# A two-layer decoder trunk with expert retrieval: TensorE adds up each batch of v rows one tick later

## The chip, the core and the metric

The kernel runs on one core of a Trainium2 chip. The metric is the device time of one execution in microseconds (us), lower is better. All data are float32.

## What is computed

The reference runs `DEPTH` = 2 layers over one sequence of 256 tokens of width 1024. A layer has a mixing half (normalisation, one input projection, three groups of attention heads, an output projection) and an expert half, the part that this case is about:

```
def peer_ffn(h, wq, subkeys, u_tab, v_tab):
    ...
        q = (hc @ wq).reshape(PEER_CHUNK, PEER_HEADS, 2, PEER_HALF)
        s = jnp.einsum('thcd,hcnd->thcn', q, subkeys).astype(jnp.float32)
        sv, si = lax.top_k(s, PEER_TOPK)
        ...
        fv, fpos = lax.top_k(cand, PEER_TOPK)
        eidx = jnp.take_along_axis(cidx, fpos, axis=-1)
        gate = jax.nn.softmax(fv, axis=-1)
        u = jnp.take(u_tab, eidx, axis=0)
        act = jnp.einsum('thkd,td->thk', u, hc).astype(jnp.float32)
        coef = (gate * jax.nn.gelu(act, approximate=False)).astype(hc.dtype)
        vsel = jnp.take(v_tab, eidx, axis=0)
        return jnp.einsum('thk,thkd->td', coef, vsel)
```

Each token picks 16 of 16,384 experts for each of 8 heads, 128 in all. An expert has a row u and a row v of 1024 numbers. The output of a token is the sum of its 128 v rows, each weighted by gate x gelu(u . h).

## The kernel before

**Phases, ticks and rows.** The 256 tokens are two tiles of 128, so there are `PHASES` = 4 phases, one for each layer and tile. The first 300 us compute the modulation vectors and the mixing half of phase 0. From then on the engines do the expert half of phase `ph` and, beside it, the mixing half of phase `ph + 1`. A phase has 64 ticks, each of `BATCH` = 2 rows. A "row" k is one gathered transfer: for each of the 128 tokens of the tile the u and the v of its k-th expert, 128 x 2048 float32, 1,048,576 bytes. In this text "tick 72" counts through all phases (phase 1 is ticks 64 to 127), and "weigh 72" is the TensorE work on the rows of tick 72.

**The ring.** Rows land in `ringmem`, a ring of 9 slots. GpSimd (POOL) issues them in order (L368), each as soon as its slot is free: row k uses the slot of row k - 9. What a row goes through: it lands; VectorE (DVE) multiplies u with h and sums (`row`, L1418, 1.2 us); after both rows of the tick ScalarE (ACT) applies gelu (L1015); DVE multiplies with the gate (L1431); ACT builds two diagonal matrices, one a row (L1023, semaphore `diag_ready`); TensorE (PE) multiplies each with its v row and adds it up in PSUM (`weigh`, L760, two matmuls a row). The last of these frees the slot.

**The mixing half beside it** is cut into 79 segments. `pace()` deals them out over the ticks from the numbers in `COST`; tick m does the segments up to `PACE[m]`. Each engine has its own list of what it does in a segment, written as a generator and moved on by `Pace.upto`. Every engine runs strictly in program order. The order inside a tick is, on DVE: two `row`s, part of a retrieval, the segments of the tick, the coefficients; on ACT: gelu, the segments, the diagonals; on PE: the segments, then `weigh` of the same tick. At tick 0 of a phase there is no segment, in phase 3 there are next to none.

The segments fall in four stretches of a phase: ticks 1 to 19 the input projection (L401, L404), whose weight groups SP loads one by one when PE is through with the group before the last (L311); ticks 19 to 36 attention and the pairwise products (L471, L484 to L552), with many round trips between PE and DVE inside a tick; ticks 37 to 48 the state sums (L585 to L614) and the output projection (L623); ticks 49 to 60 the queries (L636) and scores (L648). At the last tick PE also puts the next tile's h into PSUM (`place_h`, L750), for which it waits until DVE is done with all dot products of the phase. At tick 0 DVE takes the sums of the phase before out of PSUM (`add_sum`, L1439), for which it waits for the last weigh of that phase.

Of the kernel before, what the change touches and what calls it, by code (L numbers as in the profile page):

```python
# [38 lines left out]
TICKS = SEL // BATCH  # L39
PHASES = DEPTH * NT  # L40
# [97 lines left out]
def trunk(nc, x, c, final_norm_g, ada_pairs, w_groups, w_pieces, param_cols, param_rows, lora_w, subkeys_t, peer_uv,  # L138
# [4 lines left out]
    with ExitStack() as ctx:  # L143
# [123 lines left out]
        def slot(k):  # L267
            return ringmem[:, (ADA_SLOTS + k) % RING, :]
# [5 lines left out]
        def freed(k):  # L274

            q = ADA_SLOTS + k
            return slot_free[q % RING], q // RING + 1
# [16 lines left out]
        with nc.Block() as block:  # L294
# [78 lines left out]
            def _(pe):  # L373
# [365 lines left out]
                def last_gate():  # L739
                    for n in range(2):  # L740
                        yield 75 + n
                        gate_row(g_at(PHASES, n), gdiag[1], bank[6],
                                 ("g_sb", g_at(PHASES, n)) if n else ("q_sb", at("q_sb", PHASES, 0)))

                def place_h(ph):

                    if ph:
                        pe.wait_ge(s["dots_done"], TICKS * ph)
                    for k in range(KD):
                        tr = nc.tensor.transpose(hrep[:, k * P:(k + 1) * P], hT[:, k, :], ident)  # L750
                    tr.then_inc(s["hrep_out"], 1)

                def weigh(n):
                    pe.wait_ge(s["diag_ready"], n + 1)
                    if n % TICKS == 0 and n:
                        pe.wait_ge(s["sums_taken"], n // TICKS)
                    for k in range(n * BATCH, (n + 1) * BATCH):
                        for b in range(2):
                            q = slice(b * 512, (b + 1) * 512)
                            mm = nc.tensor.matmul(acc[:, q], diag[:, k % DIAGS, :], slot(k)[:, D:][:, q],  # L760
                                                  start=(k % SEL == 0), stop=(k % SEL == SEL - 1), skip_group_check=True)
                        mm.then_inc(freed(k)[0], 1)
# [3 lines left out]
                for ph in range(PHASES):  # L766
                    beside = Pace(mixing(ph + 1) if ph + 1 < PHASES else last_gate())
                    for m in range(TICKS):
                        beside.upto(PACE[m])
                        if m == TICKS - 1 and ph + 1 < PHASES:  # L770
                            place_h(ph + 1)
                        weigh(ph * TICKS + m)

            @block.scalar
            def _(act):
# [15 lines left out]
                def mixing(i):  # L791
# [24 lines left out]
                    def take(name):  # L816
                        g = NUMBER[name]
                        _, _, w, kind = GROUPS[g]
                        act.wait_ge(s["proj_out"], at("proj_out", i, g + 1))
                        src = group_bank(g)[:, 0:w]  # L820
                        if name == "dq":

                            for a in range(2):
                                ins = nc.scalar.activation(dq[:, a].rearrange("p j c -> p (j c)"), src, ACT.Copy,
                                                           scale=const["halves"][:, a:a + 1])
                            ins.then_inc(s["proj_sb"], 1)
                            return
                        if name in SHIFTED:
                            a, b = SHIFTED[name]
                            dst = colsT[:, a:b, 1:]  # L830
                        else:
                            dst = places[name]
                        if kind == "f":
                            src = src.rearrange("p (j c) -> p j c", c=P)
                        nc.scalar.activation(dst, src, ACT.Copy).then_inc(s["proj_sb"], 1)
# [719 lines left out]
```

## Time and profile before

| | |
|---|---|
| median of 3 runs (lowest to highest) | 1921.21 us (1920.2 to 1927.48) |
| the profiled execution | 1921.61 us |
| its span, first to last instruction | 1919.8 us |
| busy: PE / DVE / ACT / POOL | 85% / 74% / 34% / 27% |
| read from memory | 703.64 MB, 367 GB/s over the span |

The profiled execution lies 0.4 us above the median. Its phases begin with the dot products at about 307, 735, 1158 and 1585 us: three phases with mixing beside them take some 425 us each, and the last, without it, 325 us.

### The profile page before, as it was taken

How to read it: one execution, taken by the hardware profiler on the slowest of the kernel's cores; microseconds unless marked ns; L12 is line 12 of the kernel's file. 1: busy time of each engine (PE TensorE's matmuls, PEld its weight loads, DVE VectorE, ACT ScalarE, POOL GpSimd, SP SyncE). 2: the span in 40 equal slices, each digit the busy share in tenths (PEclk: the TensorE clock that was granted, in tenths of full speed). 3: DMA queues.
4: the chain of work that ended last, by engine and by line, in shares of the span. 5: the costliest groups of instructions: out<-in, count | busy, mean ns of one | idle time of the engine just before them, and what ended most of it. 6: DMA issues, size and time to landing. Idle time of an engine off the chain costs nothing.

```text
span 1919.8 us, 20976 instructions
## 1 busy us (share of the span) xinstructions
PE 1627.2 (85%) x6868; PEld 1017.1 (53%) x6868; DVE 1429.6 (74%) x3407; ACT 656.2 (34%) x1591; POOL 514.3 (27%) x564
## 2 busy tenths in 40 slices
PE   0768686998999997998999998998999998887786
PEld 0757674564556664564665664654565663333332
DVE  5768578866998666867997757868987758777754
ACT  1222123433543333433642334334642333222222
POOL 2000003222232332232232232222223333433331
PEclk9888688999999999999999999999999998999999
DMA  9963688998799999999799999998799999999995
GB/s 392 407 275 115 235 326 329 405 406 333 257 364 383 421 422 399 408 414 353 274 392 390 420 421 401 401 418 296 268 375 407 420 421 418 421 421 421 420 419 245
DMA packets 96989, 706.08 MB, mean 368 GB/s; under 512 B 10992, under 2 KB 11504, under 8 KB 13296
## 3 DMA queue, kind: packets, MB, share of 16 engines
q0 software_dynamic: 80640, 587.24, 76.6%
q1 hardware_dynamic: 16240, 117.50, 15.1%
q8 instruction: 55, 0.90, 0.2%
q14 instruction: 54, 0.44, 0.1%
HBM read 703.64 MB, written 1.05 MB: 367 GB/s over the span
## 4 chain that ended last, share of the span: by engine, by line
PE 44%; DVE 30%; DMA 18%; issue 5%; ACT 3%; POOL 0%; DVEq 0%; ACTq 0%; POOLq 0%
PE psum L760 24%; DMA ringmem<-in_peer_uv_dram,eidx 13%; DVE ringmem L1418 7%; PE psum L401 6%; PE psum L636 4%; DMA W<-in_w_groups_dram 3%; PE psum L623 3%; DMA ringmem<-in_ada_pairs_dram 2%; PE psum L404 2%; DVE ringmem L1052 2%; DVE W L1182 1%; PE psum L736 1%; ACT diag L1023 1%; DVE attn L1192 1%; DVE ast L1193 1%
## 5 line engine op out<-in xcount | busy, mean ns | idle before, releaser
L760 PE MATMUL psum<-ringmem,diag 128*128 128x512 f32 x2048 | 974.4, 623 | 124.8 <-ACT diag L1023 124.5
L368 POOL DMA_INDIRECT ringmem<-in_peer_uv_dram,eidx x512 | 488.6, 954 | 1132.3 <-PE psum L760 1086.5
L1418 DVE SCALAR_TENSOR_TENSOR ringmem<-ringmem,psum 128x1024 f32<-128x1024 f32 x512 | 613.2, 1220 | 176.6 <-DMA ringmem<-in_peer_uv_dram,eidx 162.9
L760 PEld LDWEIGHTS psum<-ringmem,diag 128*128 128x128 f32 x2048 | 391.2, 199 | 594.0 <-issue 413.0
L1023 ACT ACTIVATE diag<-K,coef 128x128 f32<-128x128 f32 x512 | 176.3, 392 | 255.3 <-DVE coef L1431 255.2
L401 PE MATMUL psum<-hT,W 128*128 128x128 f32 x1344 | 170.0, 284 | 44.3 <-DVE hT L1144 20.4
L401 PEld LDWEIGHTS psum<-hT,W 128*128 128x128 f32 x1344 | 166.8, 200 | 68.7 <-issue 41.4
L1015 ACT ACTIVATE coef<-dots 128x2 f32<-128x2 f32 x256 | 51.8, 202 | 369.6 <-DVE ringmem L1418 365.0
L1052 DVE SCALAR_TENSOR_TENSOR ringmem<-ringmem,diag 128x1024 f32<-128x1024 f32 x96 | 115.8, 1224 | 23.2 <-DMA pcols<-in_param_cols_dram 13.4
L636 PEld LDWEIGHTS psum<-hT,W 128*128 128x128 f32 x1024 | 123.3, 197 | 11.7 <-issue 7.7
L636 PE MATMUL psum<-hT,W 128*128 128x128 f32 x1024 | 126.1, 281 | 2.3 <-ACT hT L809 2.3
L1431 DVE SCALAR_TENSOR_TENSOR coef<-coef,ginv,gexp 128x2 f32<-128x2 f32 x256 | 56.7, 221 | 74.8 <-ACT coef L1015 68.5
L1015 ACT ACT_TABLE_LOAD x80 | 102.6, 1283 | 1.4
L359 POOL DMA_DIRECT2D ringmem<-in_ada_pairs_dram x48 | 25.5, 537 | 242.5 <-DVE ringmem L1052 241.7
L854 ACT ACTIVATE attn<-attn,ast 128x128 f32<-128x128 f32 (+1 forms) x64 | 28.7, 449 | 122.9 <-DVE ast L1194 122.9
L623 PE MATMUL psum<-W,hT 128*128 128x256 f32 x256 | 60.6, 394 | 2.0 <-issue 2.0
L623 PEld LDWEIGHTS psum<-W,hT 128*128 128x128 f32 x256 | 50.4, 198 | 15.9 <-issue 9.1
L383 PE MATMUL psum<-K,hm 128*128 128x128 f32 x96 | 15.4, 313 | 39.1 <-ACT hm L804 27.6
L985 ACT ACTIVATE ar<-psum 128x256 f32<-128x256 f32 x32 | 12.3, 383 | 103.9 <-PE psum L636 97.4
L404 PE MATMUL psum<-W,hT 128*128 128x260 f32 (+1 forms) x128 | 40.9, 465 | 6.0 <-DMA W<-in_w_groups_dram 6.0
L1165 DVE TENSOR_TENSOR W<-psum,K 128x512 f32<-128x512 f32 x24 | 16.6, 691 | 37.2 <-PE psum L471 36.7
L1418 DVE DVE_READ_ACCUMULATOR ringmem<-ringmem,psum 128x1 f32 x512 | 42.3, 83 | 0.0
(245 smaller groups left out, 1652.1 us busy)
## 6 DMA issues: line engine op xcount, KB each, us to landing
ringmem<-in_ada_pairs_dram POOLq DMA_DIRECT2D x48, 1024.0 KB
W<-in_w_pieces_dram SPq DMA_DIRECT2D x48, 1024.0 KB
W<-in_w_groups_dram SPq DMA_DIRECT2D x24, 1536.0 KB
W<-in_w_groups_dram SPq DMA_DIRECT2D x12, 1024.0 KB
ringmem<-in_peer_uv_dram,eidx POOLq DMA_INDIRECT x512
W<-in_w_groups_dram SPq DMA_DIRECT2D x4, 1040.0 KB
attn<-in_subkeys_t_dram SPq DMA_DIRECT2D x4, 1024.0 KB
K<-in_consts_dram SPq DMA_DIRECT2D x1, 1546.0 KB, 19.1
```

Of the source, the lines that this page charges most:

```text
L368: nc.gpsimd.indirect_dma_start(slot(k), None, rows, bass.IndirectOffsetOnAxis(ap=eidx[:, ph % 2, m:m + 1], axis=0)).then_inc(row_landed[q ...
L401: mm = nc.tensor.matmul(group_bank(g)[:, j * P:(j + 1) * P], wt[:, k, j * P:(j + 1) * P], hT[:, k, :], start=(k == 0), stop=(k == KD - 1))
L404: mm = nc.tensor.matmul(group_bank(g)[:, 0:w], hT[:, k, :], wt[:, k, 0:w], start=(k == 0), stop=(k == KD - 1))
L623: mm = nc.tensor.matmul(bank[6 + j // 2][:, (j % 2) * 256:(j % 2 + 1) * 256], hT[:, k, :], wpiece[j % 3][:, k, :], start=(k == 0), stop=(k ...
L636: mm = nc.tensor.matmul(bank[6 + h % 2][:, a * P:(a + 1) * P], wpiece[j % 3][:, k, a * P:(a + 1) * P], hT[:, k, :], start=(k == 0), stop=( ...
L760: mm = nc.tensor.matmul(acc[:, q], diag[:, k % DIAGS, :], slot(k)[:, D:][:, q], start=(k % SEL == 0), stop=(k % SEL == SEL - 1), skip_grou ...
L854: ins = nc.scalar.activation(sc[:, n % 2, a, 0:nk], sc[:, n % 2, a, 0:nk], exp, bias=ast[:, n % 2, a:a + 1], scale=DIFF_SCALE if kind == " ...
L1015: nc.scalar.activation(coef[:, q], dots[:, q], gelu).then_inc(s["gelu_out"], 1)
L1023: ins = nc.scalar.activation(diag[:, k % DIAGS, :], ident, ACT.Copy, scale=coef[:, j:j + 1])
L1052: ins = v.scalar_tensor_tensor(out=u, in0=u, scalar=1.0, in1=crow, op0=ALU.mult, op1=ALU.mult, accum_out=MC[:, l, SECTIONS[r // KD], r % K ...
L1418: ins = v.scalar_tensor_tensor(out=u, in0=u, scalar=1.0, in1=hrep, op0=ALU.mult, op1=ALU.mult, accum_out=dots[:, j:j + 1])
L1431: step(v.scalar_tensor_tensor(out=coef[:, q], in0=coef[:, q], scalar=ginv[:, ph % 2, h:h + 1], in1=gexp[:, ph % 2, m * BATCH:(m + 1) * BAT ...
```

## The change

The call of `weigh` takes the rows of the tick before, so that on PE the rows of tick n are added up behind the segments of tick n + 1. The last weigh of all comes behind the loop.

```diff
                         beside.upto(PACE[m])
                         if m == TICKS - 1 and ph + 1 < PHASES:
                             place_h(ph + 1)
-                        weigh(ph * TICKS + m)
+                        if ph or m:
+                            weigh(ph * TICKS + m - 1)
+                weigh(PHASES * TICKS - 1)
```

On PE, at the start of phase 0, the program before has this (L750 is `place_h`, L760 x4 one weigh, L383 and L401 the segments of tick 1 and on):

```order
 L750 MATMUL psum<-K,hT 128x128 x8
 L760 MATMUL psum<-ringmem,diag 128x512 x4
 L383 MATMUL psum<-K,hm 128x128 x8
 L401 MATMUL psum<-hT,W 128x128 x8
 L760 MATMUL psum<-ringmem,diag 128x512 x4
```

and the changed one this:

```order
 L750 MATMUL psum<-K,hT 128x128 x8
 L383 MATMUL psum<-K,hm 128x128 x8
 L401 MATMUL psum<-hT,W 128x128 x8
 L760 MATMUL psum<-ringmem,diag 128x512 x4
 L401 MATMUL psum<-hT,W 128x128 x8
```

The first L760 row has gone from before L383 to behind L401. From here on every place of a weigh holds the one with the next lower number: no row moves, each L760 row stands for the tick before. With the waits shown this can be seen where a phase ends. Before, on PE at the end of phase 0 (the weigh that also waits for `sums_taken` is the first one of a phase):

```order
 L760 MATMUL psum<-ringmem,diag 128x512 [waits diag_ready]
 L760 MATMUL psum<-ringmem,diag 128x512 x3
 L750 MATMUL psum<-K,hT 128x128 [waits dots_done]
 L750 MATMUL psum<-K,hT 128x128 x7
 L760 MATMUL psum<-ringmem,diag 128x512 [waits diag_ready]
 L760 MATMUL psum<-ringmem,diag 128x512 x3
 L760 MATMUL psum<-ringmem,diag 128x512 [waits sums_taken,diag_ready]
 L760 MATMUL psum<-ringmem,diag 128x512 x3
 L383 MATMUL psum<-K,hm 128x128 [waits score_sb,h_ready]
 L383 MATMUL psum<-K,hm 128x128 x7
```

and after the change:

```order
 L750 MATMUL psum<-K,hT 128x128 [waits dots_done]
 L750 MATMUL psum<-K,hT 128x128 x7
 L760 MATMUL psum<-ringmem,diag 128x512 [waits diag_ready]
 L760 MATMUL psum<-ringmem,diag 128x512 x3
 L760 MATMUL psum<-ringmem,diag 128x512 [waits diag_ready]
 L760 MATMUL psum<-ringmem,diag 128x512 x3
 L383 MATMUL psum<-K,hm 128x128 [waits score_sb,h_ready]
 L383 MATMUL psum<-K,hm 128x128 x7
 L401 MATMUL psum<-hT,W 128x128 [waits w_in0,hT_dve,hT_act]
 L401 MATMUL psum<-hT,W 128x128 x7
 L760 MATMUL psum<-ringmem,diag 128x512 [waits sums_taken,diag_ready]
```

Behind `place_h` there now stand the last two weighs of the old phase, and the first of the new one (`sums_taken`) stands behind L383 and L401. The other engines' programs are as they were.

## Rows read from the trace of the kernel before

**Rows 1.** The page's groups: the weigh's matmuls, and the row transfers' issues.
```profile
L760 PE MATMUL psum<-ringmem,diag 128*128 128x512 f32 x2048 | 974.4, 623 | 124.8 <-ACT diag L1023 124.5
L368 POOL DMA_INDIRECT ringmem<-in_peer_uv_dram,eidx x512 | 488.6, 954 | 1132.3 <-PE psum L760 1086.5
```

**Rows 2.** Stretches: length, busy us of PE, PEld, DVE, ACT, POOL; granted clock; DMA share; GB/s.
```profile
868.00:964.00 96.00, 88.08 (x369) 52.77 (x370) 82.95 (x220) 50.99 (x115) 26.31 (x28) 0.95 0.85 310
...
1012.00:1160.00 148.00, 139.37 (x596) 87.04 (x595) 101.61 (x243) 44.75 (x121) 45.18 (x48) 0.99 1.01 414
1160.00:1176.00 16.00, 9.56 (x22) 4.07 (x20) 9.12 (x23) 6.16 (x13) 3.75 (x4) 0.79 1.02 423
1176.00:1184.00 8.00, 7.38 (x41) 5.39 (x42) 7.29 (x20) 3.38 (x9) 1.87 (x2) 1.00 0.83 311
...
1600.00:1900.00 300.00, 236.26 (x495) 96.25 (x494) 214.27 (x502) 77.07 (x219) 110.10 (x117) 0.93 1.01 418
```

**Rows 3.** DVE's waits for PE's first pair products, at 430:600, 860:1010, 1290:1430.
```profile
DVE W L1165 <- PE psum L471: 8.0, 2, 6.0
...
DVE W L1165 <- PE psum L471: 6.2, 2, 4.2
...
DVE W L1165 <- PE psum L471: 7.4, 2, 5.3
```

**Rows 4.** The chain of waits, 740 to 870 us: start, us, what.
```profile
804.24 5.40 PE psum L760 x8
...
859.00 9.19 DMA W<-in_w_groups_dram
```

**Rows 5.** PE in order of time, ticks 101 to 104 of phase 1.
```profile
992.05 3.60 PE L760 MATMUL psum<-ringmem,diag 128*128 128x512 f32 x8
...
1003.74 3.60 PE L760 MATMUL psum<-ringmem,diag 128*128 128x512 f32 x8
...
1012.76 3.70 PE L760 MATMUL psum<-ringmem,diag 128*128 128x512 f32 x8
1019.15 5.40 PE L760 MATMUL psum<-ringmem,diag 128*128 128x512 f32 x8 [2.68 <-ACT diag L1023]
```

**Rows 6.** POOL in order of time at the same place.
```profile
995.92 0.94 POOL L368 DMA_INDIRECT ringmem<-in_peer_uv_dram,eidx  x1 [0.51 <-PE psum L760]
1005.89 0.94 POOL L368 DMA_INDIRECT ringmem<-in_peer_uv_dram,eidx  x1 [9.04 <-PE psum L760]
```

**Rows 7.** Two stretches of 8 us at the same place, columns as in rows 2.
```profile
1000.00:1008.00 8.00, 7.80 (x35) 5.29 (x34) 7.69 (x19) 6.64 (x16) 1.32 (x2) 0.83 0.98 385
1008.00:1016.00 8.00, 8.00 (x50) 6.01 (x49) 3.44 (x9) 1.34 (x2) 1.48 (x2) 1.00 0.94 333
```

**Rows 8.** PE in order of time, from phase 1 to phase 2.
```profile
1157.25 1.09 PE L750 MATMUL psum<-K,hT 128*128 128x128 f32 x8 [1.19 <-DVE ringmem L1418]
1158.46 3.70 PE L760 MATMUL psum<-ringmem,diag 128*128 128x512 f32 x8
1167.65 6.53 PE L760 MATMUL psum<-ringmem,diag 128*128 128x512 f32 x8 [5.48 <-ACT diag L1023]
1174.01 1.04 PE L383 MATMUL psum<-K,hm 128*128 128x128 f32 x8
1176.62 2.02 PE L401 MATMUL psum<-hT,W 128*128 128x128 f32 x16 [1.58 <-ACT hT L809]
```

**Rows 9.** DVE in order of time there: the sums of phase 1 are taken.
```profile
1163.93 1.23 DVE L1439 TENSOR_TENSOR hm<-psum,grow 128x1024 f32<-128x1024 f32 x1
```

**Rows 10.** POOL in order of time there, and a transfer in the chain of waits.
```profile
1162.44 0.94 POOL L368 DMA_INDIRECT ringmem<-in_peer_uv_dram,eidx  x1 [0.78 <-PE psum L760]
1171.70 0.94 POOL L368 DMA_INDIRECT ringmem<-in_peer_uv_dram,eidx  x1 [8.33 <-PE psum L760]
...
1144.76 16.16 DMA ringmem<-in_peer_uv_dram,eidx
```

**Rows 11.** A transfer among few others: 512 KB, us from issue to landing.
```profile
diag<-in_c_dram SPq DMA_DIRECT2D x1, 512.0 KB, 4.8
```

## Prediction

> **What bounds the kernel now.** I read the page first, then the stretches, then the waits, then single engines in order of time.
>
> The page says who waits for whom: POOL, which issues the row transfers, sat idle 1132 us, 1086 of them for PE's weigh (L760), while PE waited for diagonals (ACT L1023) only 124.5 us in all [rows 1]. So rows are issued when slots come free, and the weigh frees them.
>
> The stretches say where that matters. A row of 1,048,576 bytes takes 2.49 us at the 421 GB/s or so that the transfers reach. In phase 1 the 148 us from 1012 on run at 414 GB/s with the DMA engines busy throughout, and so does nearly all of phase 3 (418) [rows 2]. There a phase can only be as fast as its bytes. From 868 to 964 us, the attention segments, DMA moves only 310 GB/s; DVE is busy 82.95 us of 96 and PE 88.08 [rows 2]: the engines are the limit, rows wait in the ring. The other two phases have the same pattern. What the change is worth is thus: how much earlier or later do slots come free at the point (about 1010 us in phase 1) from which the transfers run without a pause to the end of the phase? Time won before that point counts only if it brings the weighs forward.
>
> **The change part by part.** It removes nothing and adds no instruction. All 2048 L760 matmuls stay, and a weigh takes 3.6 us as before [rows 5]. In the program of PE every place of a weigh holds the one of the tick before.
>
> *Gain: PE no longer stops for a diagonal that is just being made.* At tick 72 PE had idled and its weigh took 5.40 us (804.24, at the lower clock for a part) instead of 3.7; behind it the chain of waits is PE alone down to the load of the last weight group (859.00, 9.19 us), after which come the first pair products [rows 4]. In the changed kernel weigh 71 stands there, which is ready, and the segments of tick 73 are done in what was idle. All projection segments behind it come some 5 to 7 us earlier (a weigh of 3.6 less before each, plus about 2 of clock), and with them that load and the pair products L471. DVE waits for these 8.0, 6.2 and 7.4 us, 21.6 in three phases, 7.2 a phase [rows 3]. This is the most that can be won there: after it DVE is the limit.
>
> *Nothing in the attention segments.* There PE's segment of a tick needs DVE's results of the same tick, so the place of each weigh stays where it is in time. Only its number changes: slots come free a tick later. Rows have landed long before they are used there (310 of 421 GB/s), which covers it.
>
> *Loss 1: the start of phases 1 and 2.* Before, weigh 128 starts at 1167.65, after a wait of 5.48, takes 6.53 at the lower clock, and fits in front of the turn L383 (1174.01), which is held up by the new tile's normalisation anyway [rows 8]; the granted clock of that stretch is 0.79 [rows 2]. Now it stands behind L383 and L401, in the place at 1176.62 + 1.9 = 1178.5. Besides, `place_h` (ends 1158.3) now precedes two weighs instead of one, so weigh 127 ends at 1158.3 + 2 x 3.6 = 1165.5, and DVE, which takes the sums at 1163.93 without waiting [rows 9], starts 1.6 us later; the place of weigh 128 becomes 1180.1. Its first row frees a slot after half of it, at 1181.9 or so, instead of 1171.7 [rows 10]: 10 us later. The queue of transfers does not cover all of this. The row issued at 1144.76 lands 16.16 later, at 1160.9 [rows 10]; the seven issued after it up to 1162.44 last 7 x 2.49 us more, to 1178.3. The next would be issued at 1182, and a transfer needs about 3.5 us beside its own bytes (estimate from 512 KB in 4.8 us, of which 1.25 are the bytes [rows 11]), so bytes flow again at 1185.5: 7.2 us dry. Before, 1176 to 1184 ran at 311 GB/s, that is 2.1 us dry [rows 2]. Net 5.1 us less of row traffic, in a stretch that otherwise runs full, so the rows of the projection ticks come up to 5.1 us later, and DVE reaches the pair products that much later. The PE path (1.6 us for the sums, some 2 for L401 at the lower clock) is shorter and runs beside it. Bounds: 0, if rows wait long enough in the ring, and 10, the whole delay of the issue. I take 5.1, and the same for phase 0, where the first weigh moves likewise. So DVE enters the attention segments at -7.2 + 5.1 = -2.1 us, between -7.2 and +2.8.
>
> *Loss 2: the end of the light stretch.* At ticks 101 to 104 the places of the weighs are far apart: 992.05, 1003.74, 1012.76, then 1019.15 after an idle 2.68 [rows 5]. POOL had no slot from 996.9 to 1005.89, 9.04 us [rows 6], and yet the transfers kept going (385 and 333 GB/s from 1000 to 1016, together 2.4 us dry [rows 7]): what was issued at 995.92 came in front of the gap. In the changed kernel weigh 101 is in the place of 1003.74 and weigh 102 in that of 1012.76. The two rows that went out just before the gap come only behind it, and the queue runs out about 2 x 2.49 us before its former end of 1008, near 1003; with an issue at 1005.9 bytes flow at 1009.4. That is 6.4 us dry where 0.7 were, 5.7 more. At 1016 weigh 103 follows at once and the spacing is nearly as before; from here on the transfers run full to the end of the phase, so the 5.7 is not won back. Bounds: 0, if weight loads fill the hole, and 9.0, the whole gap of POOL. I take 5.7. By the same amount as DVE is early, this place is early.
>
> By row, a phase changes by -2.1 + 5.7 = +3.6 us, and three by +10.8. Phase 3 has no segments between its weighs, its order is the same and it is bound by bytes. 1921.6 + 10.8 = 1932.4; I put 1933.
>
> The Trainium skill (DMA: Bandwidth & Descriptors, Anatomy of one DMA, SWDGE path) gives a transfer a fixed cost of about 2.0 us beside its bytes. By that each dry spell would be 1.5 us shorter, a phase +0.6, and the sum 1923. The only comparable row here has 3.5, on another queue and at the start of the kernel; no row shows a lone gathered transfer.
>
> **The rivals.**
>
> *No change worth measuring.* The gain is whole and the first loss is covered (rows of ticks 68 to 74 lie waiting in the ring), so a phase is -7.2 + 5.7 = -1.5, or both halves are smaller: 1917 to 1927, say 1922. For it: a full ring holds 22 us of traffic. Against it: DMA runs full over the projection ticks, so what is lost there isn't made up before the attention segments.
>
> *Faster.* DVE's 21.6 us of waits go, and the hole at 1003 is filled by the output projection's weight loads, which SP issues when PE gets there, earlier than before: 1921.6 - 21.6 = 1900; with a half of it 1911. It decides if rows issued at 995.92 and before aren't what keeps DMA busy up to 1008. Against it: in the 16 us from 1000 to 1016 those loads were there too, and 2.4 us stayed dry.
>
> *Much slower: the ring is too short throughout.* Slots are held a tick (425/64 = 6.6 us) longer, of the 16.16 that a row now takes from issue to landing [rows 10] some 9.5 are left, and where the weighs come in uneven steps the queue empties again and again. The full stretches are three phases of 425 us, each less the 144 from 868 to 1012, 843 us at about 414 GB/s [rows 2]; if they fell to the 385 GB/s of the eight us before the gap at 1008 [rows 7], that would be 843 x (414/385 - 1) = 63 us, 1985; half of it 1953. The Trainium skill (Perfetto Trace Analysis, Identifying Performance Opportunities) says that gaps which repeat can mean too few buffers, which is this case. Against it: a queue of 16 us is nearly three times what a transfer seems to need (3.5 + 2.49), and PE's places are some us early.
>
> **How the numbers follow.** I give 0.45 to the forecast (its own range 1926 to 1942), 0.25 to no change (1917 to 1927), 0.12 to faster (1900 to 1914) and 0.18 to much slower (1943 to 1985). The range leaves out the faster half of the third and the slower half of the last: 1910 to 1953. About 0.5%, 9.6 us, is what a measurement of this kernel can tell from no change. From the cases: above 1930.8 the last case and two thirds of the first, 0.18 + 0.31 = 0.49, and a little of the second, 0.5; below 1911.6 0.11 and a little more from the second, 0.13; the rest 0.37.
>
> **What the profile after would show.** Right: PE's waits for ACT L1023 before L760 fall well below 124.5 us; DVE's waits for L471 nearly vanish; at the starts of phases 1 and 2 L383 comes without a weigh before it and POOL has a gap of 15 us or more; the 16 us about the weighs 101 to 103 move less than 385 and 333 GB/s, and dot products of ticks 114 to 128 wait for transfers as before. POOL's time without a slot grows. Wrong: if GB/s over the full stretches fell everywhere, the ring rival holds; if these stretches are as full as before and begin earlier, the gain was whole. What would upset the sum most is the first loss: if DVE enters the attention segments 7 us earlier, the whole comes out near no change.

## The result, and the profile after

The changed kernel takes 1964.81 us (median of 4 runs, 1961.01 to 1972.42), the kernel before 1922.24 beside it (4 runs, 1920.2 to 1927.48): a ratio of 1.0233, with a 95% interval of 1.021 to 1.0257, slower. The prediction was 1933, within 1910 to 1953. It had the sign at even odds and the size wrong: 11 us were forecast, 43 came.

The profiled execution has a span of 1959.2 us (before: 1919.8). In the changed kernel lines behind L771 have numbers higher by 2: L1420 is the dot product L1418, L1025 the diagonals L1023, L1441 the sums L1439, L806 and L811 are L804 and L809. The trace has two records for each matmul of a weigh, so its four stand as x8. From the changed kernel's page, the groups that answer to [rows 1], and the dot products (columns: busy us, mean ns | idle us ahead, and what ended most of it):

```profile
L760 PE MATMUL psum<-ringmem,diag 128*128 128x512 f32 x2048 | 959.2, 616 | 66.4 <-ACT diag L1025 66.3
L1420 DVE SCALAR_TENSOR_TENSOR ringmem<-ringmem,psum 128x1024 f32<-128x1024 f32 x512 | 616.3, 1220 | 292.1 <-DMA ringmem<-in_peer_uv_dram,eidx 285.2
L368 POOL DMA_INDIRECT ringmem<-in_peer_uv_dram,eidx x512 | 489.9, 957 | 1178.4 <-PE psum L760 1124.0
```

PE waits for diagonals half as long as before, 66.3 us, and all of that lies in phase 3: from 300 to 1600 us, where it was 63.1 in the kernel before, the wait is gone. Another has grown: DVE's dot products wait 285.2 us for rows (162.9 in the kernel before), and POOL sits idle 46 us longer ahead of its issues, of which 37.5 are put down to a slot that PE has not freed.

Stretches of the changed kernel, columns as in [rows 2]. The first three are the state sums and what follows them in phase 1, from tick 103 on (answering to [rows 7] and the 148 us of [rows 2]), the next three the start of phase 2, the last is in phase 3:

```profile
1012.00:1028.00 16.00, 15.74 (x92) 12.70 (x93) 9.40 (x24) 7.98 (x17) 1.86 (x2) 0.89 0.79 303
1028.00:1036.00 8.00, 6.56 (x16) 2.62 (x14) 7.58 (x17) 2.48 (x5) 3.73 (x4) 1.00 0.99 391
1036.00:1184.00 148.00, 134.82 (x574) 85.85 (x575) 93.65 (x227) 42.05 (x116) 42.92 (x45) 0.97 0.99 404
...
1184.00:1200.00 16.00, 6.18 (x19) 3.28 (x17) 8.26 (x20) 5.31 (x11) 3.39 (x4) 0.73 0.98 407
1200.00:1208.00 8.00, 6.42 (x25) 4.66 (x24) 7.31 (x21) 3.93 (x10) 0.67 (x1) 0.69 0.01 4
1208.00:1216.00 8.00, 8.00 (x46) 5.66 (x45) 5.60 (x13) 2.36 (x7) 3.08 (x4) 1.00 0.86 306
...
1635.00:1935.00 300.00, 231.03 (x488) 94.51 (x487) 214.49 (x511) 76.20 (x216) 112.03 (x118) 0.94 1.01 419
```

Measured against 421 GB/s, the start of phase 2 is dry for 0.5 + 7.9 + 2.2 = 10.6 us. For eight of them nothing moves at all (4 GB/s). The 24 us from 1012 on are dry for 4.5 + 0.6 us, and the 148 us after it run at 404 where they ran at 414. Phase 3 is as full as before (419 and 418).

PE in order of time from phase 1 to phase 2, answering to [rows 8]:

```profile
1172.23 8.00 PE L760 MATMUL psum<-ringmem,diag 128*128 128x512 f32 x16
1180.56 1.09 PE L750 MATMUL psum<-K,hT 128*128 128x128 f32 x8 [0.33 <-DVE ringmem L1420]
1181.49 7.03 PE L760 MATMUL psum<-ringmem,diag 128*128 128x512 f32 x16
1198.34 1.97 PE L383 MATMUL psum<-K,hm 128*128 128x128 f32 x8 [9.82 <-ACT hm L806]
1201.88 3.46 PE L401 MATMUL psum<-hT,W 128*128 128x128 f32 x16 [1.58 <-ACT hT L811]
1205.18 3.60 PE L760 MATMUL psum<-ringmem,diag 128*128 128x512 f32 x8
```

POOL in order of time there, answering to [rows 10]:

```profile
1188.79 0.94 POOL L368 DMA_INDIRECT ringmem<-in_peer_uv_dram,eidx  x1 [0.78 <-PE psum L760]
1207.33 0.94 POOL L368 DMA_INDIRECT ringmem<-in_peer_uv_dram,eidx  x1 [17.61 <-PE psum L760]
```

and DVE, answering to [rows 9]:

```profile
1188.61 1.23 DVE L1441 TENSOR_TENSOR hm<-psum,grow 128x1024 f32<-128x1024 f32 x1 [1.42 <-issue]
```

Behind the two weighs of the old phase PE idles 9.82 us, and then L383 takes 1.97 us (1.04 before) and L401 3.46 (2.02 before), with a granted clock of 0.69 in the stretch. Only then comes the weigh of the new phase. POOL had no slot for 17.61 us.

How the lag grows can be read off the starts of the dot products in DVE's order of time. The table gives, for the first dot product of some ticks, how much later than in the kernel before it starts (us; negative is earlier), in one profiled execution each, with the difference at tick 0 taken off. The kernels beside the changed one are those of the experiments.

| tick | changed | e4, first weigh late | e7, place_h first | e3, 37 to 62 late | e11, 2 to 21 late | e15, 7 slots |
|---|---|---|---|---|---|---|
| 8 | +6.9 | +6.5 | 0.0 | 0.0 | -2.9 | +5.3 |
| 36 | -1.7 | +6.1 | -0.1 | -0.2 | -11.8 | +6.2 |
| 64 | +9.3 | +5.5 | +0.9 | +14.4 | -12.1 | +16.9 |
| 72 | +19.1 | +11.6 | +4.1 | +13.4 | -13.6 | +20.6 |
| 84 | +19.6 | +12.9 | +4.8 | +13.4 | -14.8 | +27.8 |
| 100 | +13.2 | +11.9 | +3.7 | +12.1 | -21.0 | +27.2 |
| 128 | +26.0 | +11.3 | +4.2 | +24.6 | -20.0 | +43.7 |
| 136 | +35.2 | +17.9 | +8.8 | +23.0 | -21.2 | +46.4 |
| 164 | +29.7 | +18.3 | +9.9 | +23.8 | -28.0 | +57.9 |
| 192 | +36.1 | +16.5 | +5.9 | +33.8 | -27.9 | +67.5 |
| 255 | +39.6 | +16.5 | +9.4 | +35.2 | -28.4 | +79.2 |

In the changed kernel each phase gains 5 to 9 us in its attention ticks and ahead of them (8 to 36: -8.6, 84 to 100: -6.4, 136 to 164: -5.5), loses 7 to 10 at its start (0 to 8: +6.9, 64 to 72: +9.8, 128 to 136: +9.2), and 6 to 13 from tick 36 to its end (36 to 64: +11.0, 100 to 128: +12.8, 164 to 192: +6.4). These are three quantities, and the experiments take them one by one. "us by ratio" below is the measured ratio less 1, times 1920; the 95% interval of each such number reaches some 3 to 6 us to either side (10 for e15).

### The profile page after: what moved, and what is told of

The parts are those of the page before. It is cut to its first block, busy times and chain, and to the rows that moved or that the text cites. A ratio compares the mean times of both kernels' runs of the same rounds, so it can differ in the third digit from the quotient of the medians.

```text
span 1959.2 us, 20976 instructions
## 1 busy us (share of the span) xinstructions
PE 1625.6 (83%) x6868; PEld 1023.7 (52%) x6868; DVE 1429.8 (73%) x3407; ACT 654.9 (33%) x1591; POOL 515.6 (26%) x564
## 3 DMA queue, kind: packets, MB, share of 16 engines
q1 hardware_dynamic: 16240, 117.50, 14.8%
## 4 chain that ended last, share of the span: by engine, by line
PE 46%; DVE 25%; DMA 22%; issue 4%; ACT 3%; POOL 0%; DVEq 0%; ACTq 0%; POOLq 0%
PE psum L760 24%; DMA ringmem<-in_peer_uv_dram,eidx 19%; DVE ringmem L1420 6%; PE psum L401 5%; PE psum L636 5%; PE psum L623 3%; DVE ringmem L1054 2%; DMA ringmem<-in_ada_pairs_dram 2%; PE psum L404 2%; DMA W<-in_w_groups_dram 2%; PE psum L736 1%; DVE attn L1194 1%; DVE ast L1195 1%; DVE W L1167 1%; DVE W L1184 1%
## 5 line engine op out<-in xcount | busy, mean ns | idle before, releaser
L760 PE MATMUL psum<-ringmem,diag 128*128 128x512 f32 x2048 | 959.2, 616 | 66.4 <-ACT diag L1025 66.3
L1420 DVE SCALAR_TENSOR_TENSOR ringmem<-ringmem,psum 128x1024 f32<-128x1024 f32 x512 | 616.3, 1220 | 292.1 <-DMA ringmem<-in_peer_uv_dram,eidx 285.2
L760 PEld LDWEIGHTS psum<-ringmem,diag 128*128 128x128 f32 x2048 | 388.9, 198 | 523.9 <-issue 413.9
L1025 ACT ACTIVATE diag<-K,coef 128x128 f32<-128x128 f32 x512 | 176.4, 392 | 286.1 <-DVE coef L1433 285.9
L401 PE MATMUL psum<-hT,W 128*128 128x128 f32 x1344 | 172.0, 286 | 42.3 <-DVE hT L1146 20.4
L401 PEld LDWEIGHTS psum<-hT,W 128*128 128x128 f32 x1344 | 169.1, 202 | 66.6 <-issue 41.1
L636 PEld LDWEIGHTS psum<-hT,W 128*128 128x128 f32 x1024 | 123.3, 197 | 15.1 <-ACT hT L811 7.9
L383 PE MATMUL psum<-K,hm 128*128 128x128 f32 x96 | 19.9, 375 | 92.6 <-ACT hm L806 74.6
L383 PEld LDWEIGHTS psum<-K,hm 128*128 128x128 f32 x96 | 15.7, 193 | 100.0 <-ACT hm L806 56.9
L1420 DVE DVE_READ_ACCUMULATOR ringmem<-ringmem,psum 128x1 f32 x512 | 42.3, 83 | 0.0
## 6 DMA issues: line engine op xcount, KB each, us to landing
ringmem<-in_peer_uv_dram,eidx POOLq DMA_INDIRECT x512, 11.2
```

Of the source, the lines that this page charges most:

```text
L383: tr = nc.tensor.transpose(bank[4 + b][:, j * P:(j + 1) * P], hm[:, (4 * b + j) * P:(4 * b + j + 1) * P], ident)
L401: mm = nc.tensor.matmul(group_bank(g)[:, j * P:(j + 1) * P], wt[:, k, j * P:(j + 1) * P], hT[:, k, :], start=(k == 0), stop=(k == KD - 1))
L636: mm = nc.tensor.matmul(bank[6 + h % 2][:, a * P:(a + 1) * P], wpiece[j % 3][:, k, a * P:(a + 1) * P], hT[:, k, :], start=(k == 0), stop=( ...
L1025: ins = nc.scalar.activation(diag[:, k % DIAGS, :], ident, ACT.Copy, scale=coef[:, j:j + 1])
L1420: ins = v.scalar_tensor_tensor(out=u, in0=u, scalar=1.0, in1=hrep, op0=ALU.mult, op1=ALU.mult, accum_out=dots[:, j:j + 1])
```

## The experiments

All but two of these kernels keep the order of the segments and change only which weighs are late. The loop of the changed kernel is written with a count of the weighs done, so that late ones are caught up where the condition ends:

```diff
+                added = [0]
...
+                        n = ph * TICKS + m
+                        late = ph < PHASES - 1 and 8 <= m <= 21
                         if m == TICKS - 1 and ph + 1 < PHASES:
                             place_h(ph + 1)
-                        weigh(ph * TICKS + m)
+                        while added[0] < (n if late else n + 1):
+                            weigh(added[0])
+                            added[0] += 1
```

**e1, the end and the start of a phase as before.** Here and in e3 and e6 the last tick also does the weigh that is still open ahead of `place_h`:

```diff
+                        late = ph < PHASES - 1 and 1 <= m <= 62
+                        if m == TICKS - 1:
+                            weigh(added[0])
+                            added[0] += 1
```

> The changed order inside a phase (ticks 1 to 62 late), but the end and the start of a phase as before: weigh 62 ahead of place_h, weigh 63 behind it, and the new phase's first weigh ahead of L383. Theory A (the price is paid at places: some 10.5 us a phase at its start, 11.5 from the end of the pair products to the phase's end, against a gain of 7 to 8): 1965 less 3 x 10.5 = 1933, within 1926 to 1942. Theory B (the ring is short by a tick everywhere, so the price is spread over all ticks with late weighs): 2 of 64 ticks are restored, 1960 to 1965.

Measured: 1936.38 us, ratio 1.0091 (1.0061 to 1.012), +17 by ratio. Theory A's number. Of the 45 us that the change costs by ratio, 28 go with the few instructions at the phases' borders (and with phase 3, where e1 has no late weigh), the other 17 with all the rest.

**e2, only the projection late.** `8 <= m <= 21`, as in the diff above.

> Only weighs of ticks 8 to 21 of phases 0 to 2 are a tick late (the input projection); all others stand as before. Theory A: the whole gain at the pair products, 7 to 8 us a phase, and neither loss: 1922 less 22 = 1900, within 1896 to 1908. Theory B: the gain less 14 of 64 parts of some 21 us a phase, 4.6, so 1913. Theory C (the gain does not come from these ticks): 1922.

Measured: 1894.6 us, ratio 0.9868 (0.9843 to 0.9893), -25 by ratio, 8.4 a phase. The whole gain stands by itself, a little more than expected, and the kernel is faster than both the changed one and the one before. DVE's waits for L471 are gone. They are not all of the gain: in phase 0 the dot products are 3.5 us early at tick 20 already, ahead of the pair products, and 11.2 at tick 36. A stretch of phase 1's projection ticks reads

```profile
777.00:854.00 77.00, 72.34 (x333) 47.84 (x332) 59.26 (x149) 24.57 (x62) 20.90 (x22) 0.98 1.01 420
```

The transfers run at 420 GB/s there (before, 409 from 1185 to 1291 and 411 from 764 to 868).

**e3, only ticks 37 to 62 late** (`37 <= m <= 62`, and the last tick as in e1).

> Only weighs of ticks 37 to 62 of phases 0 to 2 are late (state sums, output projection, queries, scores), with the end and start of a phase as before. Theory A: 11.5 us a phase are lost there, 1922 + 34 = 1956, within 1946 to 1960. The sum of the prediction had 5.7 a phase: 1939. Theory B: 26 of 64 parts of 21 us a phase, 8.5, so 1948.

Measured: 1959.4 us, ratio 1.02 (1.0173 to 1.0228), +38 by ratio, 12.8 a phase. Theory A, at the upper end of its range; the 5.7 a phase in the sum of the prediction are less than half of it. Two stretches of phase 1:

```profile
1020.00:1028.00 8.00, 8.00 (x51) 6.09 (x50) 4.95 (x16) 5.72 (x11) 1.87 (x2) 1.00 0.49 146
...
1050.00:1190.00 140.00, 130.63 (x553) 81.93 (x551) 85.00 (x210) 39.27 (x108) 42.64 (x45) 0.96 1.00 410
```

A hole of 5.2 us (8 x (1 - 146/421)) behind the late weighs' first ticks, and then 140 us that are nearly but not quite full, 3.7 us in all. The last of these ticks are where it shows: in the kernel before, the 100 us ahead of phase 2 run at 420 GB/s,

```profile
1058.00:1158.00 100.00, 94.38 (x453) 60.71 (x452) 63.78 (x159) 34.40 (x93) 31.83 (x34) 1.00 1.01 420
```

and in e3 the last 55 us ahead of it at 402:

```profile
1134.00:1189.00 55.00, 50.03 (x199) 29.63 (x199) 26.06 (x53) 15.41 (x46) 17.53 (x19) 0.94 1.00 402
```

**e4, only the first weigh of each phase late** (`late = m == 0`).

> Only the first weigh of each phase is late: it stands behind L383 and the first L401, with the second tick's weigh behind it; all else as before. Theory A: nearly the whole loss at a phase's start, three starts of 7 to 10 us with mixing beside them: 1943 to 1952. The sum of the prediction had 5.1 a phase: 1937. Theory B: one tick of 64, 1923.

Measured: 1942.5 us, ratio 1.0109 (1.0078 to 1.0141), +21 by ratio, 7.0 a phase. Four matmuls, moved behind sixteen or so others three times over, cost 1.1%. The value lies between the prediction's term (5.1) and the 7 to 10 that the changed kernel loses at each start. PE in order of time at the start of phase 2:

```profile
1173.14 3.70 PE L760 MATMUL psum<-ringmem,diag 128*128 128x512 f32 x8
1188.32 1.97 PE L383 MATMUL psum<-K,hm 128*128 128x128 f32 x8 [11.48 <-ACT hm L809]
1191.87 3.75 PE L401 MATMUL psum<-hT,W 128*128 128x128 f32 x16 [1.58 <-ACT hT L814]
1195.41 7.96 PE L760 MATMUL psum<-ringmem,diag 128*128 128x512 f32 x16
```

POOL in order of time there:

```profile
1177.12 0.94 POOL L368 DMA_INDIRECT ringmem<-in_peer_uv_dram,eidx  x1 [0.78 <-PE psum L760]
1198.50 0.94 POOL L368 DMA_INDIRECT ringmem<-in_peer_uv_dram,eidx  x1 [20.45 <-PE psum L760]
```

and three stretches, columns as in [rows 2]:

```profile
1184.00:1192.00 8.00, 2.10 (x9) 1.73 (x9) 1.76 (x7) 5.44 (x10) 0.00 (x0) 0.50 0.86 357
1192.00:1200.00 8.00, 8.00 (x25) 5.50 (x26) 6.57 (x18) 3.08 (x7) 0.94 (x1) 0.67 0.01 2
1200.00:1208.00 8.00, 8.00 (x31) 4.45 (x30) 2.25 (x5) 1.08 (x3) 3.66 (x4) 1.00 0.99 359
```

Dry: 1.2 + 8.0 + 1.2 = 10.4 us. The prediction had 7.2, but 1.6 of these were for sums taken late behind `place_h`, which e4 leaves where it was; its number for e4 is 5.6. Of the 4.8 between them 4.0 can be read off the rows: with no weigh ahead of it PE idles 11.48 us, and then L383 takes 1.97 for 1.04, L401 3.75 for 2.02, and the first slot is free 3.1 us after the weigh's start instead of the 1.8 reckoned. The granted clock in these rows is 0.50 and 0.67. POOL's slots run out at 1178.06, yet the transfers go on into the stretch of 1184 to 1192: the queue drains first.

**e5, a ring of 8 slots** (`RING = 8`, the kernel before otherwise).

> The kernel before with a ring of 8 slots instead of 9; nothing else. It prices one slot, that is half of what the change holds back. Theory A (slots only matter where the weighs come in uneven steps, so a slot is worth its 2.49 us of cover at the two to three dry places of a phase): 1921 + 3 x 5 to 7.5 = 1936 to 1944. Theory B (the ring is short throughout): half of the 65 us that the change loses once its gain is set aside, 1954 or more.

Measured: 1932.7 us, ratio 1.0073 (1.0058 to 1.0088), +14 by ratio. Just below theory A's 15 to 22, far from the other's 33.

**e6, only ticks 49 to 62 late** (and the last tick as in e1).

> Only weighs 49 to 62 of phases 0 to 2 are late (queries and scores); the end and start of a phase as before. With all of ticks 37 to 62 late the loss was 38 us, of which the dot products' times put some 24 ahead of tick 49 and 14 behind it. Theory A: 1921 + 14 = 1935, within 1930 to 1942. The sum of the prediction had nothing here: 1921.

Measured: 1926.88 us, ratio 1.0045 (1.0028 to 1.0062), +9 by ratio. Less than the 14 that the table of dot products had suggested, but not nothing: the queries and scores, where rows arrive just in time, have a price of their own.

**e7, place_h one weigh earlier** (`late = ph < PHASES - 1 and m == 62`).

> Only the order at a phase's end is changed: place_h (and its wait for all dot products) stands ahead of the last two weighs instead of the last one; the first weigh of the new phase is where it was. Theory A: what the whole change lost beyond the parts measured so far (1965 against 1921 - 27 + 38 + 21 = 1953, so 12) lies here in part: 2 to 3 us a phase, 1927 to 1930. The prediction had 1.6 us, hidden: 1921.

Measured: 1931.26 us, ratio 1.006 (1.0044 to 1.0076), +12 by ratio, 3.8 a phase. PE in order of time at the end of phase 1 (4.64 is the wait for all dot products of the phase):

```profile
1156.13 3.70 PE L760 MATMUL psum<-ringmem,diag 128*128 128x512 f32 x8 [1.26 <-ACT diag L1028]
1164.48 1.97 PE L750 MATMUL psum<-K,hT 128*128 128x128 f32 x8 [4.64 <-DVE ringmem L1423]
1166.24 9.12 PE L760 MATMUL psum<-ringmem,diag 128*128 128x512 f32 x16
```

DVE, which takes the sums of phase 1:

```profile
1175.45 1.22 DVE L1444 TENSOR_TENSOR hm<-psum,grow 128x1024 f32<-128x1024 f32 x1 [4.36 <-issue]
```

POOL in order of time:

```profile
1170.13 0.94 POOL L368 DMA_INDIRECT ringmem<-in_peer_uv_dram,eidx  x1 [9.09 <-PE psum L760]
...
1193.32 0.94 POOL L368 DMA_INDIRECT ringmem<-in_peer_uv_dram,eidx  x1 [9.24 <-PE psum L760]
```

and two stretches, columns as in [rows 2]:

```profile
1184.00:1192.00 8.00, 5.25 (x26) 4.59 (x27) 5.41 (x17) 4.81 (x9) 0.08 (x1) 0.79 0.66 265
1192.00:1200.00 8.00, 8.00 (x33) 4.63 (x32) 5.58 (x13) 1.98 (x6) 2.82 (x3) 1.00 0.63 230
```

`place_h` waits for the dot products, and weigh 126, which had stood in just that gap, waits behind it. After the idle 4.64 us `place_h` takes 1.97 us (1.09 in [rows 8]) and the two weighs 9.12 (one took 3.70 there), so DVE takes the sums 10.97 us behind the start of `place_h`, where it was 6.68 [rows 8, rows 9]. All that hangs on the sums comes later with them, down to the slot issued at 1193.32, 28.8 us behind the start of `place_h` instead of 23.4 (1180.64 in the kernel before). POOL waits twice. Its first wait, 9.09 us, leaves no hole: the transfers run at 407 GB/s from 1176 to 1184. The queue runs empty in front of the second, 9.24 us (5.26 in the kernel before): 3.0 + 3.6 = 6.6 us dry.

**e8, projection and attention late** (`8 <= m <= 36`).

> As the projection-only kernel (1895), and weighs 22 to 36 late as well. The prediction said that the attention segments neither gain nor lose: 1895, within 1891 to 1899. Theory B: 15 more late ticks of 64 cost 5 us a phase, 1910. Against both: if PE still stops for diagonals there, up to 3 us a phase less, 1886.

Measured: 1900.18 us, ratio 0.9911 (0.9894 to 0.9928), -17 by ratio: 8 us worse than e2. The dot products say where: against e2 it is level at tick 36 and 4.8 us behind at tick 44 (differences at tick 0 taken off), and loses 2.4 more from tick 100 to 106 and 2.7 from 164 to 177. Inside the attention ticks next to nothing is lost (at most 0.3 us a phase). It is lost behind tick 36. That the slots still held late there are the cause is not shown: e12 below has none late behind tick 26, and in phase 0 it too is behind e2 at tick 44, by 4.0 us (0.9 at tick 36), and by its time it can't be told apart from e8.

**e9, only ticks 8 and 9 late; e10, only 15 to 21; e11, 2 to 21; e12, 8 to 26** (the condition on `m` alone is changed).

> Only weighs 8 and 9 of phases 0 to 2 are late, caught up in tick 10. In the kernel before PE stops 4.20 us for a diagonal at tick 72 and its weigh then takes 1.7 longer. Theory S (that stop is the gain): 3 x 5.9 off 1919, 1901, within 1898 to 1906. Theory W (what helps is that one weigh of 3.6 fewer stands ahead of the last weight group and of L471, which needs late weighs up to tick 21): 1919.

> Only weighs 15 to 21 of phases 0 to 2 are late. Theory S: no stop of PE is avoided there, 1919. Theory W: L471 comes 3.6 us earlier a phase and DVE, which waits for it, with it: 1919 - 11 = 1908. Both causes may add: then this run and the one with weighs 8 and 9 late make up the 25 us between them.

> As the projection-only kernel (1895), but late from tick 2 on instead of tick 8. The rows of these ticks are the ones that the transfers only just bring in time. Theory A (the price is paid where the queue of transfers is at its lowest, and the ticks behind a phase's start are such a place): 2 to 3 us a phase, 1901 to 1904. Theory B (6 more late ticks of 64): 2 us a phase, 1901. Neither: 1895.

> As the projection-only kernel (1895), but late up to tick 26 instead of 21. With all ticks to 36 late, 8 us of the gain were lost. Theory A (they are lost behind tick 36, where the transfers start to run full and find slots late): 1895, within 1891 to 1898. Theory B (lost evenly over the attention ticks): 2.7, 1898.

| | us | ratio (95%) | us by ratio |
|---|---|---|---|
| e9, 8 and 9 | 1908.82 | 0.9942 (0.992 to 0.9963) | -11 |
| e10, 15 to 21 | 1902.03 | 0.9894 (0.9872 to 0.9915) | -20 |
| e11, 2 to 21 | 1889.78 | 0.9831 (0.9806 to 0.9856) | -32 |
| e12, 8 to 26 | 1899.57 | 0.9886 (0.9865 to 0.9907) | -22 |

e9 and e10 both gain: late weighs at the stop of tick 72 are worth 11 us where 18 were expected, those of the last projection ticks 20 where 11 were. Their sum, 31, is above e2's 25, but within the error of three such numbers. Neither run is as pure as its expectation has it. In e9 the stop of phase 1 is shortened, not gone: 2.45 us for 4.20, and its weigh takes 3.70 for 5.40, together 3.5, near the 3.7 a phase that e9 gains. And e10, which was to avoid no stop, avoids one. In the kernel before, PE stops again between the first two groups of pair products of phase 1:

```profile
879.70 3.70 PE L760 MATMUL psum<-ringmem,diag 128*128 128x512 f32 x8 [1.45 <-ACT diag L1023]
```

In e10 this stop is gone, and the way from the start of the L401 that waits for its weights to the second group of L471 is 11.9 us (855.38 to 867.28) instead of 15.1 (868.24 to 883.33). These 3.2 and the 3.6 of one weigh fewer make the 6.8 a phase that e10 gains; this was read in one phase only. Both kernels shorten DVE's wait for L471. It was 8.0 us in phase 0 [rows 3]; the waits of DVE in e9 have for phase 0 (us in total, times, longest)

```profile
DVE W L1170 <- PE psum L471: 5.2, 2, 3.2
```

and those of e10 for phase 1, with none in phase 0:

```profile
DVE W L1170 <- PE psum L471: 0.7, 2, 0.5
```

e11 is the surprise: all theories on record had late weighs from tick 2 cost 0 to 9 us more than e2, and it has the lowest time of all, 1889.78. Its interval overlaps that of e2, so a gain of ticks 2 to 7 isn't shown, but the 6 to 9 us of cost that two theories expected are ruled out. The rows of these ticks do not suffer from a slot that is held a tick longer. The losses at a phase's start are thus not in ticks 2 to 7 (tick 1 was not tried by itself). By its interval e12 can't be told apart from e2.

**e13, only 37 to 40 late; e14, only 41 to 48; e15, a ring of 7 slots** (`RING = 7`, the kernel before otherwise).

> Only weighs 37 to 40 of phases 0 to 2 are late: the four ticks for which the prediction worked out 5.7 us a phase, 17 in all. Theory A (the price is paid where the queue empties first, behind tick 37): 20 to 24 of the 38 us that all ticks from 37 to 62 cost, 1919 + 22 = 1941. Theory B (spread over all late ticks): 4 of 26, 1925.

> Only weighs 41 to 48 are late (ticks 37 to 40 and 49 to 62 as before). Theory A: the ring has filled up again by then, 3 us a phase at most, 1919 to 1928. Theory B: 8 of 26 ticks, 12 us, 1931. With the run for 37 to 40 (and the 9 us of 49 to 62) this says whether the 38 us are a sum of places or of ticks.

> The kernel before with a ring of 7 slots: what the ring would be if the change simply held two rows more at all times. One slot fewer cost 14 us. Theory A: holding a slot a tick longer at a place with a long gap costs more than a slot fewer everywhere; 7 slots cost 35 to 50, less than the 76 that the change costs beside its gain of 33. Theory B (the change is a ring of 7, short throughout): 1919 + 76 = 1995.

Measured: e13 1942.15 us, ratio 1.0112 (1.0095 to 1.0129), +22 by ratio; e14 1940.91, the same ratio, +22; e15 2001.24, ratio 1.0419 (1.0368 to 1.0469), +80. In e13 theory A has its number, 7.2 a phase. In e14 it hasn't: ticks 41 to 48 were to be nearly free and cost as much. With e6 the three make 52 us, while all of them together (e3) cost 38. A part of each may be the passage to late weighs itself, where one tick has no weigh and two ticks' work stand between weighs; no run takes it apart. In e13 POOL waits for a slot at this place of phase 1, in order of time, as long as this:

```profile
1014.98 0.94 POOL L368 DMA_INDIRECT ringmem<-in_peer_uv_dram,eidx  x1 [16.23 <-PE psum L760]
```

and in e14, some ticks further on:

```profile
1042.56 0.93 POOL L368 DMA_INDIRECT ringmem<-in_peer_uv_dram,eidx  x1 [10.70 <-PE psum L760]
```

e15 goes against theory A as well. The first slot taken away cost 14 us, the second 66 more, and the 80 are close to the 77 that the change costs beside the gain of e11. But the two are not the same loss, as the table of dot products shows. The ring of 7 loses 7.2 us from tick 72 to 84 and 11.7 from 192 to 255. The changed kernel loses 0.5 and 3.5 there. In phase 3 the ring of 7 has

```profile
1675.00:1960.00 285.00, 216.40 (x442) 86.14 (x442) 200.88 (x479) 68.80 (x194) 106.04 (x111) 0.93 1.00 409
```

409 GB/s, where both other kernels have 418 or 419.

## Why the prediction was wrong

**The parts add up.** By ratio: the projection ticks -32 (e11), the attention ticks +8 (e8 against e2), ticks 37 to 62 +38 (e3), the first weigh +21 (e4), `place_h` +12 (e7), together +47, against +45 for the whole change. The same inside: e1, which leaves out the last two, should be -32 + 8 + 38 = +14, and is +17. That the match is so close is in part luck. Each part has an error of 3 to 6 us, the sum of five one of some 11; with e2 in place of e11 it is +54; the parts of ticks 37 to 62 did not add up among themselves; and e7's 12 us do not carry over whole, as told below.

**The gain** was the mechanism named and nearly the size: 7.2 us a phase forecast, 8.4 (e2) to 10.8 (e11) measured. The waits for L471 vanished as foreseen. That 7.2 is the most that can be won was too strict: DVE is early ahead of that wait already (e2, 3.5 us at tick 20), in a stretch where the transfers now run at 420 GB/s.

**"Nothing in the attention segments"** failed by 2.8 us a phase, with an error of 2. The rows used there are covered, as said, and the loss appears behind tick 36; whether slots held late at tick 36 are its cause stays open, since e12 has none.

**Loss 1, the start of a phase**: 5.1 us forecast, 7 to 10 measured (the table), 7.0 for the first weigh alone (e4). The step that failed is "The PE path (1.6 us for the sums, some 2 for L401 at the lower clock) is shorter and runs beside it". That path stands ahead of the weigh, so the lower clock on L383, on L401 and on the weigh's own start delays the slot: in e4 10.4 us are dry where the same reckoning gives 5.6, in the changed kernel 10.6 where 7.2 were forecast. In the changed kernel the slot comes 26.8 us behind the start of `place_h` (1180.56 to 1207.33), not 24.7 as reckoned. `place_h` itself went as forecast there: it waits 0.33 us and takes 1.09, and the sums are taken 8.05 us behind its start, 1.4 later than before where 1.6 were put. The 3.8 a phase of e7 hold the price of an idle 4.64 us and of the low clock behind it, which the changed kernel does not have.

**Loss 2, behind the attention ticks** ("the end of the light stretch"): the term itself was near, 5.7 us a phase forecast and 7.2 measured (e13, within its bounds of 0 to 9.0). What failed is the sentence behind it, "from here on the transfers run full to the end of the phase". Ticks 41 to 62 have a price too (e14, e6), and ticks 37 to 62 as a whole cost 12.8 a phase (e3). They were put at nothing because the transfers ran full there (420 GB/s from 1058 to 1158). A full stretch says only that the queue did not run empty, not by how much; with slots a tick later it does run empty (404 in the changed kernel, 402 ahead of phase 2 in e3). This is the largest error of the sum, 7 of the 11 or so us that a phase came out above the 3.6 forecast.

**The rival that came true by its number** is "the ring is too short" (1943 to 1985), given 0.18. Its mechanism, short throughout, is half right. The kernel with 7 slots shows that two slots are indeed worth 80 us here, which no step of the sum suggested. But the changed kernel loses at places: next to nothing in the projection ticks, nothing but its start in phase 3. And its full stretch fell from 414 to 404 GB/s, not to the 385 from which that case's 1985 was worked out. The Trainium skill's rule that was weighed for the dry spells (DMA: Bandwidth & Descriptors, Anatomy of one DMA, SWDGE path: about 2.0 us beside the bytes) would have made the sum smaller still. The lone gathered transfer that the kernel before had no row for is there in the changed kernel, issued at 1207.33 into an empty queue (column: us from issue to landing):

```profile
ringmem<-in_peer_uv_dram,eidx POOLq DMA_INDIRECT x1, 5.6
```

5.6 less 2.49 for its bytes is 3.1 us beside them, nearer to the 3.5 that was taken than to the 2.0 of the Trainium skill.

The signs that the prediction named for being right are nearly all there (no waits for L471, L383 without a weigh ahead of it, a gap of 17.61 us on POOL, 303 GB/s about the state sums): the places were right, and the prices behind them too low.

**What stays open**: how the 38 us of ticks 37 to 62 divide, since late weighs in one part change what the next costs, and each part tried alone has a passage of its own; what the 8 us of the attention ticks come from; and whether ticks 2 to 7 add to the gain. No run gives the changed kernel a longer ring, which would be the most direct test of whether slots are all that it lacks.

## What to carry to other kernels

Here a ring of buffers feeds a transfer that runs full, and the time at which slots are freed decides. Of a consumer that is moved in such a kernel, ask what stands ahead of it at its new place, waits and clock included, and follow the late slot until the queue in front of it has drained: in e4 POOL had no slot from 1178.06 on, and the transfers stopped only about 12 us later. Delay it where its producer makes it stop and other work can fill the stop (here ticks 2 to 21 of 64: 1.7% faster), and leave it first in line where a long wait follows or the transfers are just full. And before a stretch is called full and safe, take a slot away: here the first cost 14 us and the second 66.

## What was not expected of the hardware

A move of four matmuls changed TensorE's granted clock for its neighbours. With the weigh ahead of them, L383 took 1.04 us and L401 2.02 [rows 8]. In e4 PE idled 11.48 us in its place, the granted clock of the eight microseconds was 0.50, that is the lower of the two levels, 1.2 GHz, and L383 took 1.97 us and L401 3.75. The slow time was there before too: the weigh that filled the gap took 6.53 us instead of 3.6. But the L383 behind it had to wait for the normalisation until 1173.60 in any case and started at 1174.01. In e4 the work behind the gap is the slow one, and it stands ahead of the weigh that frees the slots.
